# Moving eight conditioning pieces from the first attention to the end of the recurrent stage

## The reference, cut to what matters

```python
for i in range(DEPTH):                                   # 2 layers
    mx = split((silu_c  @ ada_w[i] + ada_b[i]), 6)       # for x
    mc = split( silu_cc @ ada_w[i] + ada_b[i],  6)       # for ctx
    h_x = modulate(rms_norm(x, g[0]), mx[0], mx[1])
    y_x = attention_mixer(...) if i == 0 else rglru_mixer(...)
    x = x + mx[2] * rms_norm(y_x, g[1])
    x = x + mx[5] * rms_norm(sqrelu_mlp(modulate(rms_norm(x, g[2]), mx[3], mx[4]), mlp_w1[i], mlp_w2[i]), g[3])
```

## Time and profile before

| what | us |
|---|---|
| median of 3 runs | 1676.56 (1670.72 to 1677.47) |
| the profiled execution: its own time | 1678.59 |
| its span, first to last instruction | 1676.9 |
| PE busy | 1563.2 (93%) |
| DVE busy | 1103.0 (66%) |
| ACT busy | 846.2 (50%) |

### The profile page before, as it was taken

One profiled execution on the slowest core, in us unless ns is written; L12 is line 12 of the kernel. 1 busy time (PEld: TensorE's weight loads), 2 busy tenths in 40 slices (PEclk: granted clock), 3 DMA queues, 4 the chain that ended last, 5 costly groups with the idle time before them and its releaser, 6 DMA issues.

```text
span 1676.9 us, 23997 instructions
## 1 busy us (share of the span) xinstructions
PE 1563.2 (93%) x8710; PEld 1285.3 (77%) x8710; DVE 1103.0 (66%) x1741; ACT 846.2 (50%) x1349; POOL 14.0 (1%) x36
## 2 busy tenths in 40 slices
PE   6989989999999999999779999988887899999999
PEld 4855548988888889887569998875666788889788
DVE  3446654854444448699986667875663779687895
ACT  4325545733222227788674445544241657566572
POOL 2000000000000000000010000000000000000000
PEclk9999999999999999999899999997998899999999
DMA  9388732423233232333345665442220579788792
GB/s 346 95 332 295 276 152 76 151 76 96 92 100 100 88 100 76 101 100 103 124 137 178 188 187 163 139 138 80 72 75 0 201 266 369 262 304 320 248 369 97
DMA packets 195800, 279.70 MB, mean 167 GB/s; under 512 B 12434, under 2 KB 111220, under 8 KB 190588
## 3 DMA queue, kind: packets, MB, share of 16 engines
q1 hardware_dynamic: 194308, 274.21, 48.4%
q0 software_dynamic: 1152, 4.19, 0.7%
q10 hardware_dynamic: 248, 0.09, 0.0%
HBM read 277.40 MB, written 1.05 MB: 166 GB/s over the span
## 4 chain that ended last, share of the span: by engine, by line
PE 73%; DVE 14%; ACT 6%; issue 4%; DMA 2%; SPq 1%; DVEq 0%; ACTq 0%
PE bank L435 64%; DVE weights_lo L408 3%; ACT weights_hi L396 2%; PE bank L736 1%; PE bank L1346 1%; PE bank L1330 1%; DMA ada_rows_in<-in_ada_w_dram 1%; PE bank L1314 1%; ACT work L2071 1%; DVE softmax_cols L2582 1%; DMA stage<-in_w_in_dram 1%; DVE work L2573 1%; DVE work L2715 1%; DVE x_and_ctx L582 1%; PE bank L1731 1%
## 5 line engine op out<-in xcount | busy, mean ns | idle before, releaser
L408 DVE TENSOR_TENSOR weights_lo<-stage,weights_hi 128x1024 fp32r<-128x1024 f32 x332 | 394.6, 1220 | 70.9 <-ACT weights_hi L396 67.3
L396 ACT ACTIVATE weights_hi<-stage 128x1024 fp32r<-128x1024 f32 x332 | 338.0, 1055 | 156.0 <-PE bank L435 104.2
L435 PE MATMUL bank<-act_hi,weights_hi 128*128 128x256 f32 (+1 forms) x1040 | 326.4, 314 | 3.3 <-DVE weights_lo L408 2.8
L435 PE MATMUL bank<-act_lo,weights_hi 128*128 128x256 f32 (+1 forms) x1040 | 324.6, 312 | 0.0
L435 PE MATMUL bank<-act_hi,weights_lo 128*128 128x256 f32 (+1 forms) x1040 | 324.5, 312 | 0.0
L435 PE MATMUL bank<-weights_hi,ff_hi 128*128 128x512 f32 x560 | 220.2, 393 | 4.3 <-DVE ff_lo L2927 1.9
L435 PE MATMUL bank<-weights_hi,ff_lo 128*128 128x512 f32 x560 | 219.8, 392 | 0.0
L435 PE MATMUL bank<-weights_lo,ff_hi 128*128 128x512 f32 x560 | 219.4, 392 | 0.0
L435 PE MATMUL bank<-weights_hi,act_hi 128*128 128x512 f32 (+1 forms) x488 | 197.1, 404 | 20.2 <-DVE act_lo L2780 12.7
L435 PEld LDWEIGHTS bank<-act_hi,weights_hi 128*128 128x128 f32 x1040 | 199.9, 192 | 16.9 <-DVE weights_lo L408 3.7
L435 PEld LDWEIGHTS bank<-act_lo,weights_hi 128*128 128x128 f32 x1040 | 200.0, 192 | 11.1
(11 more groups left out here) (393 smaller groups left out, 1990.0 us busy)
## 6 DMA issues: line engine op xcount, KB each, us to landing
stage<-in_mlp_w_dram SPq DMA_DIRECT2D x128, 512.0 KB, 4.0
stage<-in_w_dram SPq DMA_DIRECT2D x96, 512.0 KB, 6.1
ada_rows_in<-in_ada_w_dram SPq DMA_DIRECT2D x40, 1024.0 KB, 5.6
x_and_ctx<-in_w_dram SPq DMA_DIRECT2D x48, 512.0 KB, 6.0
work<-in_w_dram SPq DMA_DIRECT2D x48, 512.0 KB, 6.4
stage<-in_w_in_dram SPq DMA_DIRECT2D x32, 512.0 KB, 4.1
stage<-in_lru_w_in_dram SPq DMA_DIRECT2D x20, 512.0 KB, 3.8
stage<-in_attn_w_qkv_dram SPq DMA_DIRECT2D x12, 512.0 KB, 8.1
```

The costliest lines, as they stand in the source:

```text
L396: act.eng.activation(whi[u % NRING][:], landing(act, u)[:], ACT.Copy).then_inc(sem("hi_ready"), 1)
L408: dve.eng.tensor_tensor(wlo[u % NRING][:], landing(dve, u)[:], whi[u % NRING][:].bitcast(F32), ALU.subtract).then_inc(sem("lo_ready"), 1)
L435: m = pe.eng.matmul(ps, l, r, start=start and j == 0, stop=stop and j == 2, skip_group_check=True)
```

## The change

The eight pieces of pair 5 are no longer taken in the attention. They become sixteen half pieces of 128 x 1024 (512 KB), loaded by POOL into four places that are free at the end of the recurrent stage, and multiplied four at a time after each of the first four pairs of output units. `ADA_STEPS` becomes one piece a step up to h = 26 and none after; five pieces are taken ahead of the attention, around `turn_qk(2)`; `turn_qk(1)` moves into `qkv(2)`; half of "g0a" is spread earlier. In the recurrent stage ACT and DVE split two units more in their first block and none or two fewer later, the input gate of the last block gets a buffer of its own (`lru_last_i`), `lru_out(0..3)` go between the other work, and "g1b" is spread after the first hidden products of the MLP.

```diff
-                      "n1b": ([0, 1, 2, 3],), ...
+                      "n1b": ([4, 5, 6, 7],), ...
@@ ada_pe
-                if p >= 48:
-                    return
@@
+        LATE_FREE = 2 * [84 + 26] + 2 * [84 + 28]
+        def late_rows(i):
+            return [ada_in[3][:, 512:1536], ada_in[5][:, 512:1536], ada_in[0][:, 1024:2048],
+                    ada_in[1][:, 1024:2048]][i % 4]
+        def late_load(e):                                   # runs on POOL
+            for i in range(16):
+                m, k = 4 + i // 8, i % 8
+                if i < 4:
+                    e.wait_ge(sem(USED), LATE_FREE[i])
+                else:
+                    e.wait_ge(sem("late_used"), i - 3)
+                e.dma_start(late_rows(i), ada_w[1, k * P:(k + 1) * P, m * D:m * D + D]).then_inc(
+                    sem(f"late_in{i % 4}_full"), 16)
+        def late_pe(pe, bank, first):
+            for i in range(first, first + 4):
+                half, k = i // 8, i % 8
+                ...
+                pe.eng.wait_ge(sem(f"late_in{i % 4}_full"), 16 * (i // 4 + 1))
+                for q in range(4):
+                    m = pe.eng.matmul(psum[bank][32 * q:32 * q + 32, half * 256:half * 256 + 256],
+                                      adastat[:, k, :], late_rows(i)[:, q * 256:q * 256 + 256], ...)
+                m.then_inc(sem("late_used"), 1)
+        def late_dve(dve):                                  # four small additions of the bias
+            dve.eng.wait_ge(*dve.filled(("ada", 5, "cols")))
+            ...
@@ attention
-        ADA_STEPS = [1, 1, 1, 1, 2, 2] + [1, 1, 1, 1, 2, 2] + [1, 1, 1, 1, 1, 1, 2] + [1, 1, 1, 1, 2, 2] + [1, 1, 1, 1, 1, 1, 2]
-        ADA_TURN = {5: 1, 11: 2, 18: 3, 24: 4, 31: 5}
+        ADA_AHEAD = (4, 1)
+        ADA_STEPS = 27 * [1] + 5 * [0]
+        ADA_TURN = {2: 1, 10: 2, 18: 3, 26: 4}
+        LAST_I = [tbuf[:], U[1]]
@@ SP
+                    if n == 1 and kq == 2:
+                        ada_load(sp, 8, 10)
-                        ada_load(sp.eng, 8, 48)
+                        ada_load(sp, 10, 40)
@@ PE, projections and attention
+                    if n == 2 and kq == 1:                  # inside qkv(2)
+                        turn_qk(1)
             qkv(2)
-            turn_qk(1)
+            ada_pe(pe, 7, ADA_AHEAD[0])
             turn_qk(2)
+            ada_pe(pe, 7, ADA_AHEAD[1])
-                if h == 32:
-                    spread_pe(pe, "g0a", colG, 2, [0, 1, 2, 3], ("gate_col", 1))
                 if h >= 3 and h % 2:
                     values((h - 3) // 2)
+                if h == 31:
+                    spread_pe(pe, "g0a", colG, [0], [0, 1, 2, 3], ("gate_col", 1))
+                    ada_pe(pe, 7, ADA_STEPS[h])
+                if h == 32:
+                    spread_pe(pe, "g0a", colG, [1], [0, 1, 2, 3], ("gate_col", 1))
                 if 1 <= h < 33:
                     turn_probs(h - 1)
@@ PE, end of the recurrent stage (output banks 0 to 3 in place of 4 to 7)
+                late_pe(pe, 4, 4 * kp)                      # after each kp in 0..3
-            spread_pe(pe, "g1a", colG, 1, [0, 1], ("gate_col", 3))
-            spread_pe(pe, "g1b", colH, 1, [2, 3], ("gate_col", 4))
+            spread_pe(pe, "g1a", colG, [0], [5, 6], ("gate_col", 3))
+            ada_cols_pe(pe, 5, 4)
             ...
+            spread_pe(pe, "g1b", colH, [0], [6, 7], ("gate_col", 4))   # after hidden_pe of m1f
@@ ACT
-                split_hi(act, 2 if n == 0 else 4)
+                split_hi(act, 4)                            # lru_a
+            def lru_last_i():
+                n = RB - 1
+                s.wait_ge(sem("u_used"), n)
+                for md in range(4): ...                     # sigmoids of ("i", 4, md) into LAST_I
             def lru_b(n):
                 for m, kind, dst, col in (...):
+                    if n == RB - 1:
+                        if kind == "i":
+                            continue
+                        split_hi(act, 2)
                     if n and kind == "a":
                         s.wait_ge(sem("lru_sum"), 2 * n - 1 + m)
-                split_hi(act, 2 if n < RB - 2 else 6 if n == RB - 2 else 4)
+                if n == RB - 2:
+                    lru_last_i()
+                else:
+                    split_hi(act, 2 if n < RB - 2 else 4)
             s.wait_ge(sem("u_used"), RB)
+            ada_act(act, 5)
             spread_act(act, "g1a", rows_1[:, 0:1, :], 1)
-            spread_act(act, "g1b", rows_1[:, 1:2, :], 1)    # now after m1f's hidden_act
@@ DVE
-            gate_col(colH, 1, 5, 3)                         # before the MLP of layer 0
-            cols(1, 3, 2, "norm_col")                       # before the recurrent stage
-                split_lo(dve, 2 if n == 0 else 4)
+                split_lo(dve, 4 if n < RB - 1 else 0)       # lru_conv
-            (the loop shown above)
+            for n in range(RB - 1):
+                lru_conv(n + 1)
+                if n == RB - 2:
+                    lru_out(0)
+                    split_lo(dve, 2)
+                lru_d1(n)
+                if n < RB - 2:
+                    split_lo(dve, 2)
+                lru_d2(n)
+            split_lo(dve, 2)
+            lru_out(1)
+            lru_d1(RB - 1)                                  # waits for lru_decay 20
+            lru_out(2)
+            split_lo(dve, 2)
+            lru_out(3)
+            split_lo(dve, 2)
+            lru_d2(RB - 1)
+            lru_out(RB - 1)
+            split_lo(dve, 2)
+            late_dve(dve)
+            cols(1, 3, 2, "norm_col")
+            gate_col(colH, 1, 5, 3)
+            v.wait_ge(*dve.own())
             split_lo(dve, 2)
@@ POOL
+            late_load(g)
             g.wait_ge(*tile_at("n1b", "x", 0))
```

More of the change, by code:

```diff
@@ L637, in ring_before, with ada_load @@
             return max(u for u in range(12) if u % NRING // 2 == pair) + 1
-        def ada_load(g, first, end):
+        def ada_load(sp, first, end):
+            g = sp.eng
             for p in range(first, end):
@@ L742, in ada_pe @@
                 pe.ada += 1
+        LATE_FREE = 2 * [84 + 26] + 2 * [84 + 28]
[14 more added lines that the diff above has]
+                half, k = i // 8, i % 8
+                if i == 0:
+                    pe.eng.wait_ge(*pe.bank_free(bank))
+                    pe.take(("ada", 5), bank)
+                pe.eng.wait_ge(sem(f"late_in{i % 4}_full"), 16 * (i // 4 + 1))
+                for q in range(4):
+                    m = pe.eng.matmul(psum[bank][32 * q:32 * q + 32, half * 256:half * 256 + 256], adastat[:, k, :],
+                                      late_rows(i)[:, q * 256:q * 256 + 256], start=k == 0, stop=k == 7,
+                                      skip_group_check=True)
+                m.then_inc(sem("late_used"), 1)
+            plan.entry[("ada", 5)]["full"] = ("late_used", 16)
+        def late_dve(dve):
+            dve.eng.wait_ge(*dve.filled(("ada", 5, "cols")))
+            ps = plan.bank(("ada", 5, "cols"))
+            v = ps[:, 0:32].rearrange("p (m j q w) -> p w m q j", m=2, j=2, q=4)
+            for w in range(2):
+                for m in range(2):
+                    dst = MC[:, 1, 4 + m, :, w].rearrange("p (q j) -> p q j", q=4)
+                    bias = params[:, 0, 48 + (4 + m) * 8:48 + (5 + m) * 8].rearrange("p (q j) -> p q j", q=4)
+                    i = dve.eng.tensor_tensor(dst, v[:, w, m], bias, ALU.add)
+                    if w + m < 2:
+                        i.then_inc(*dve.mark())
+            i.then_inc(*dve.free(("ada", 5, "cols")))
+            dve.eng.wait_ge(*dve.own())
         def ada_cols_pe(pe, pair, bank):
@@ L769, in ada_dve, with spread_pe @@
             i.then_inc(*dve.free(("ada", pair, "cols")))
-        def spread_pe(pe, key, col, n_who, banks, ready):
+        def spread_pe(pe, key, col, whos, banks, ready):
             pe.eng.wait_ge(*pe.at(*ready))
-            for w in range(n_who):
+            for w in whos:
                 for half in range(2):
@@ L2231, in _ @@
                 split_hi(act, 2 if m == 3 else 1)
+            spread_act(act, "g1b", rows_1[:, 1:2, :], 1)
             split_hi(act, 2)
@@ L2735, in lru_conv @@
                                 ALU.subtract).then_inc(*dve.mark("u_split"))
-                split_lo(dve, 2 if n == 0 else 4)
+                split_lo(dve, 4 if n < RB - 1 else 0)
             def lru_d1(n):
+                if n == RB - 1:
+                    for md in range(4):
+                        v.wait_ge(*dve.freed(("i", n, md)))
+                    for m in range(2):
+                        v.tensor_tensor(I[:, 2 * m:2 * m + 2, :], LAST_I[m],
+                                        U[n % 2][:, m, :].unsqueeze(1).to_broadcast([P, 2, 512]),
+                                        ALU.mult).then_inc(*dve.mark("u_used" if m else None))
+                    v.wait_ge(*dve.own())
+                    v.wait_ge(sem("lru_decay"), 4 * n + 4)
```

(26 more changed lines are left out.)

23 lines of the change are left out of this document (14 added, 9 removed).

## The result

| | before | after |
|---|---|---|
| median | 1676.56 (11 runs, 1670.72 to 1679.28) | 1681.42 (11 runs, 1678.49 to 1686.83) |
| ratio, 95% interval | | 1.0039 (1.0027 to 1.0051) |
| profiled execution: own time, span | 1678.59, 1676.9 | 1680.54, 1678.7 |

The change made the kernel slower: by 4.9 us from median to median, by 4.5 to 8.6 us (middle 6.5) by the ratio. The forecast of 1674.8 had the wrong sign; the range to 1682 holds the median, and 0.39% lies within the 0.5% to which 0.72 was given.

A forecast was written before the change was run, and what follows sets the result against it. It took DVE's beat to bound the attention, and DVE, busy 48.8 of 52.2 us, the recurrent stage's end. Attention -9.7, blocks 0 to 3 -0.1 and recurrent end +8.0 gave -1.8 off 1676.56: 1674.8, range 1666 to 1682.

The forecast's parts named there:

- start of the attention: First scores start 0.5 us sooner and keep the full clock: 1.5 us gained, 0.5 if the clock falls.
- first sixteen steps: Attention's first half: no doubled pieces, two turnings of a pair stay; 3.6 us gained, 2.5 without slack.
- last sixteen: Attention's second half: doubled steps go, turnings and the split of two weight units stay; 1.1 us gained (0.5 to 2.2).
- tail: Attention's end: half of "g0a" spread earlier, so the last transposes come sooner; 3.5 us gained (3.0 to 3.8).
- blocks 0 to 3: Recurrent stage before its last block: two more units split in block 0, in waits of both engines; 0.1 us gained.
- end of the recurrent stage: Late splits and loads make ACT and DVE wait, and the squares come later: 8.0 us lost (5.4 to 10.5).
- Its end, DVE: Recurrent stage's end: DVE stands 8 us for the decays behind late loads; last `lru_out` ends at 843.6, before 841.87.
- The attention: Whole attention, from start, both halves and tail together: 9.7 us gained (6.5 to 12.0).
- Attention doesn't get shorter: DVE sets the attention's beat, doubled steps hardly count, only start and tail gain: total +3, 1679.5; chance 0.10.
- Late halves arrive late: Recurrent end: POOL's half pieces land late and hold PE's last pair; total +5 to +8, 1683; chance 0.12.
- tail hidden: Recurrent end: ACT never stands for units 120/121 and 126/127, PE sets the end; -8 to -12, about 1666.5; chance 0.18.
- three signs of being wrong: No wait at ACT's `lru_b(4)` splits; PE waiting over 2 us for `late_in`; first-half attention beats keeping their excess.

The follow-up runs named there:

- e9: Changed kernel, but POOL issues the second four half pieces only once ACT has split unit 121; median 1677.87, ratio to the kernel before 1.0005.
- e1: Changed kernel with ACT's split of units 120 and 121 moved behind the last block's roots, no longer ahead of its last two sigmoids; median 1673.53, ratio to before 0.9979.
- e10: Kernel before with only a new attention: all forty pieces kept, five ahead, five at step 28, half of "g0a" spread earlier; median 1669.00, ratio to before 0.9959.
- e4: Changed kernel with ACT's and DVE's recurrent-stage order taken back to that of before, half pieces kept; median 1682.82, ratio to before 1.0041.
- e5: Changed kernel with the edits of e1 and e2 together; median 1670.79, ratio to the kernel before 0.9969.
- e3: Changed kernel without the sixteen half pieces: no loads, matmuls or turning of their sums; median 1677.36, ratio to the kernel before 1.0012.
- e2: Changed kernel with DVE splitting units 122 and 123 inside the last block's scans, not behind its `lru_out`; median 1682.83, ratio to before 1.0040.
- e8: Kernel of e1 with two attention pieces moved from steps 25 and 26 to step 28; median 1672.23, ratio to the kernel before 0.9979.

## Why the prediction was wrong

By its own steps, against the earlier trace rows:

| step | predicted | measured |
|---|---|---|
| start of the attention | -1.5 | -1.46 |
| first sixteen steps | -3.6 | -2.57 |
| last sixteen | -1.1 | -1.02 |
| tail | -3.5 | -1.84 |
| blocks 0 to 3 | -0.1 | +0.36 |
| end of the recurrent stage | +8.0 | +12.31 |
| sum | -1.8 | +5.78 |

**The step that failed** is in "Its end, DVE": "Landing takes 3.5 to 5.8, median 4.6; the four late loads that POOL issues then (after 808) share the engines. I take 1.2 more." That makes 5.8 for unit 121. It was 9.59, and sharing was 5 of it and not 1.2. The mechanism was right and in its place: ACT waits for 120 and 121 ahead of two sigmoids, DVE stands at the first use of the decays, the squares wait for 127. But DVE stood 11.84 us and not 8, and as 122 is split behind `lru_out` of the last block, the load of 126 and the squares were late by the same. Counting from the low part, `lru_out` lost 5.85 (59.13 less 53.28) where 1.8 was predicted: 4 of the 4.3 us. e9 prices the sharing at 3.9, and what it leaves, 8.4 over before, is close to the 8.0 predicted; e1 prices the place of the split at 9.8. The bound of 10.5 was too low as well: two transfers with four others beside them cannot be bounded by landings without company. The prediction had a row for it: the earlier trace rows show 6.9 to 12.4 for eight loads that POOL issued between 2.3 and 21.7 us, with others in flight. I used it for POOL's loads alone, though SP's loads were in flight beside them and ran on the same DMA engines.

**The attention** was off by 2.8 in this profile (by 0.7 to 4.6 over the seven with this code). First sixteen: I gave 1.4 us of slack against the two turnings of a pair, but each made its beat 5.27 in place of 4.28, in full: 0.99 twice. With the row of the turning (1.06) and no slack the answer would have been 2.5. Tail: the order came out as predicted, but half of "g0a" took 3.30 and not 1.83, since PE had 1.2 GHz there. The prediction watched the clock at the start, where it was right (the first scores took 1.13), and not at the end, from where it had just taken PE's filling work away. That this is why it fell there is likely and not shown.

**The rivals.** "Attention doesn't get shorter" fell: the first sixteen steps gained 2.57. But the doubled steps of the first half can be spread without moving pieces out (e10). "Late halves arrive late" had the right sign and resource at the wrong victim: PE waited 0.25 us in the last round, SP's units paid; it is right for e1 and e4, where ACT's order no longer hides it. The condition of "tail hidden", no stand of ACT at 120 and 121 that counts, is met in e1, which came 3.5 us below before by its ratio and not 8 to 12, as PE then waits for half pieces.

None of the prediction's three signs of being wrong came: ACT did wait, PE waited under 2 us, and the first half lost most of its excess. They test the mechanism, and none tests the size of the landing.

## What to carry to other kernels

A queue that must wait for a transfer should have nothing behind that wait which another engine needs sooner: moving one split behind twelve other instructions of ACT, the first two of them ready, was worth 8 us of the median. When an edit adds transfers, price them at the loads of others that are in flight at that moment, not only at their own users. And before moving filler work away from a stage, try where in the same stage an engine stands idle: spread better, the forty pieces made the kernel faster (e10, 0.9959), while moving eight of them made it slower (1.0039), and with its order mended (e5, 0.9969) not faster than e10.

## What was not expected of the hardware

A 512 KB load took 3.9 to 4.7 us with one other beside it (e3, e9) and 7.0 to 9.9 with five others (after, e1, e2). And unchanged code scatters: the same stage took 65.98 and 63.74 us in two profiles (e1, e8), the same attention gained 5.1 to 9.0 us in seven, and a stretch of 211 to 216 us was granted 0.86 and 0.89, so that two profiled executions hid 4.8 of a difference of 6.6 us.
